# The shared expert's down product moves into the expert loop, and groups of one, two and four experts are spread in the loop

## The reference

```python
h = modulate(rmsnorm(x, norm2_g[l]), sh2, sc2)
idx, wts = route(h, w_router, bias)          # 64 experts, top 8 of each token
routed = sum of silu(h @ w1[e]) * (h @ w3[e]) @ w2[e], weighted, over the chosen e
shared = (silu(h @ s1) * (h @ s3)) @ s2
x = x + g2 * (shared + routed)
```

## Time and profile before

| | us |
|---|---|
| median of 3 runs | 1285.77 (1285.69 to 1286.42) |
| the profiled execution's own time | 1286.71 |
| its span in the trace | 1284.7 |
| PE busy | 1194.7 |
| DVE busy | 363.3 |
| ACT busy | 319.4 |

### The profile page before, as it was taken

The page is one execution under the profiler, slowest core; times in us unless marked ns, Lnnn a source line. Parts: engine busy times, 40 slices in busy tenths (PEclk is TensorE's granted clock), DMA queues, the critical chain, the costliest instruction groups (busy, mean ns, idle before and its releaser), DMA issues.

```text
span 1284.7 us, 16205 instructions
## 1 busy us (share of the span) xinstructions
PE 1194.7 (93%) x6220; PEld 635.2 (49%) x6220; DVE 363.3 (28%) x1140; ACT 319.4 (25%) x570; POOL 10.0 (1%) x44
## 2 busy tenths in 40 slices
PE   5999899999788899999999999999788999999996
PEld 1866447455343444455455747455334444444553
DVE  0495236222112212222124427122112212222124
ACT  1124422222212222222223212222112212222223
POOL 2000000000000000000000000000000000000000
PEclk8899999999888999999999999999889989999998
DMA  9998729899999999999999586699999999999994
GB/s 366 394 416 364 298 80 416 341 391 421 422 421 420 422 420 421 420 421 421 421 422 400 236 331 248 244 392 421 421 422 420 422 420 421 421 420 421 421 421 169
DMA packets 77533, 487.82 MB, mean 380 GB/s; under 512 B 7816, under 2 KB 8968, under 8 KB 23440
## 3 DMA queue, kind: packets, MB, share of 16 engines
q1 hardware_dynamic: 76288, 485.26, 92.1%
q10 hardware_dynamic: 1168, 1.52, 0.3%
HBM read 485.70 MB, written 1.05 MB: 379 GB/s over the span
## 4 chain that ended last, share of the span: by engine, by line
PE 71%; DMA 22%; SPq 3%; DVE 2%; ACT 1%; issue 1%; DVEq 0%; ACTq 0%
PE PS L1347 26%; DMA ring<-in_moe_w 18%; PE PS L1380 10%; PE PS L1296 7%; PE PS L1330 6%; PE PS L1392 5%; PE PS L1317 4%; PE PS L1257 3%; SPq L434 2%; DMA ring<-in_ada_w 2%; PE PS L1475 2%; DMA ring<-in_od_w_in 1%; PE PS L1537 1%; PE PS L1422 1%; PE PS L1405 1%
## 5 line engine op out<-in xcount | busy, mean ns | idle before, releaser
L1347 PE MATMUL PS<-ring,xg 128*32 128x512 f32 (+2 forms) x928 | 206.6, 633 | 26.0 <-DMA ring<-in_moe_w 25.9
L1347 PE MATMUL PS<-ring,xn 128*64 128x512 f32 (+2 forms) x992 | 206.6, 632 | 24.4 <-DMA ring<-in_moe_w 24.4
L1380 PE MATMUL PS<-ring,hidT 128*64 128x512 f32 (+2 forms) x960 | 203.7, 596 | 1.4 <-DVE hidT L1049 1.4
L1347 PEld LDWEIGHTS PS<-ring,xg 128*32 128x32 f32 (+2 forms) x928 | 71.0, 141 | 159.2 <-issue 159.2
L1347 PEld LDWEIGHTS PS<-ring,xn 128*64 128x64 f32 (+2 forms) x992 | 69.2, 137 | 158.8 <-issue 157.3
L1054 DVE SCALAR_TENSOR_TENSOR yl<-PS,wslot,yh 128x1024 fp32r<-128x1024 f32 x58 | 74.4, 1283 | 227.2 <-ACT yh L713 227.2
L1046 DVE TENSOR_TENSOR hid<-PS,hid 128x256 f32<-128x256 f32 x58 | 24.6, 425 | 365.6 <-ACT hid L703 365.6
L1330 PE MATMUL PS<-hot,xh 128*128 128x256 f32 x448 | 126.4, 315 | 1.3 <-ACT xg L689 1.3
L703 ACT ACTIVATE hid<-PS 128x256 f32<-128x256 f32 x58 | 22.3, 385 | 410.3 <-PE PS L1347 399.2
L1380 PEld LDWEIGHTS PS<-ring,hidT 128*64 128x64 f32 (+2 forms) x960 | 64.0, 133 | 99.5 <-issue 92.5
L1330 PE MATMUL PS<-hot,xl 128*128 128x256 f32 x448 | 111.4, 282 | 0.0
(11 more groups left out here) (247 smaller groups left out, 933.5 us busy)
## 6 DMA issues: line engine op xcount, KB each, us to landing
ring<-in_moe_w SPq DMA_DIRECT2D x384, 1024.0 KB, 18.5
ring<-in_ada_w SPq DMA_DIRECT2D x48, 1024.0 KB, 13.0
ring<-in_ev_w_in SPq DMA_DIRECT2D x10, 1024.0 KB, 15.9
ring<-in_sh_w SPq DMA_DIRECT2D x6, 1024.0 KB, 14.4
ring<-in_ev_w_out SPq DMA_DIRECT2D x4, 1024.0 KB, 11.7
ring<-in_od_w_in SPq DMA_DIRECT2D x4, 1024.0 KB, 16.9
ring<-in_od_w_out SPq DMA_DIRECT2D x4, 1024.0 KB, 13.9
x<-in_x SPq DMA_DIRECT2D x1, 1024.0 KB, 5.5
```

Of the source, the lines that this page charges most:

```text
L1347: ins = M(PS[o:o + rows, 6, :], xg[gp][:, k, first_slot + o:first_slot + o + rows], w13[:, :, k, :], start=(k == 0), stop=(k == KD - 1))
L1380: ins = M(PS[o:o + rows, 4 + h, :], hidT[:, m, o:o + rows], slot_view(slots[2][0], 2)[:, m, h * 512:(h + 1) * 512], start=(m == 0), stop=( ...
```

## The change

- The order of the groups becomes P P and then `QWQPPPPWPPPWQWQWWQPWPPQPPW`.
- The shared down product leaves the place before the loop and is done in one piece of 8 matmuls on PE (`shared_down`), before the `up` of group 20 (the 21st). Its tile s2 is no longer loaded before the loop. It takes a place of its own in the list of experts, with kind 2 alone, and is loaded with group 20. So a layer now has 61 places, and `RUN_CELL` becomes cells 1 to 4. The first `scatter` now starts banks 0 to 3.
- The first gather's four parts move up among the routing steps, into banks 7 and 6 in turn. One half of the split of x (`xh` for the second 128 tokens) moves from DVE to ACT. The normalisation of the weights (`weigh`) and the sort come after the first one-hot tables on DVE.
- The block counting on PE (`cumulate`, `make_list`) moves into group 0, `block_list` on DVE behind group 0, and the wait for `ctl_ready` into group 1.
- The loads of groups 2 and 3 are issued in one list, sorted by the time at which their places come free.

```diff
-    for n in range(NARROW // 4):
-        order += [[wide.pop(0)], narrow[4 * n:4 * n + 4]]
-    order += [[wide.pop(0)]]
-    order += [middle[2 * n:2 * n + 2] for n in range(len(middle) // 2)]
-    return order + [[wide.pop(0)]]
+    for kind in "QWQPPPPWPPPWQWQWWQPWPPQPPW":
+        cols, n = {"W": (wide, 1), "P": (middle, 2), "Q": (narrow, 4)}[kind]
+        order.append([cols.pop(0) for _ in range(n)])
+    return order
+SHARED_AT = 20
...
-        EXPERTS = [(g, j) for g in range(NG) for j in range(len(COLUMNS[g]))]
+        EXPERTS = [(g, j) for g in range(NG) for j in range(-(g == SHARED_AT), len(COLUMNS[g]))]
+        SHARED_N = EXPERTS.index((SHARED_AT, -1))
...
-                     + [(("shared", 1, i), NSLOT + i) for i in range(3)])
+                     + [(("shared", 1, i), NSLOT + i) for i in range(2)])
...
+            def load_groups(l, gs, prev):
+
+                who, tiles = {}, []
+                for g in gs:
+                    if g == SHARED_AT:
+                        tiles.append((SHARED_N, 2))
+                    for j, c in enumerate(COLUMNS[g]):
...
+                        tiles += [(n, kind) for kind in range(3)]
+                tiles.sort(key=lambda t: (place_free(*t) if len(gs) > 1 else 0, t[1] == 2))
+                for n, kind in tiles:
+                    s = 3 * (n % CELLS) + kind
+                    if n < CELLS:
+                        wait_occupant(prev[s])
+                    else:
+                        sp.wait_ge(*given_back(l, former(n, kind), kind))
...
-                for g in range(FIXED // 2, NG):
-                    load_group(l, g, prev)
+                load_groups(l, [2, 3], prev)
+                for g in range(4, NG):
+                    load_groups(l, [g], prev)
... ACT, in moe(l)
+                src = x[:, TC - 1, :].rearrange("p (q k) -> p k q", k=KD)
+                nc.scalar.activation(xh[:, TC - 1, :, :], src, ACT.Copy, scale=stat[:, TC - 1:TC]).then_inc(high_ready, 1)
+                load_table(ACT.Silu)
+                act.wait_ge(shared_used, 2 * l + 1)
+                nc.scalar.activation(shs, PS[:, 5, :], ACT.Silu).then_inc(shared_silu, 1)
+                f = main[l]
+                for part in range(2):
+                    gather_out(f, part + 1, 0, part, 7 - part)
                 act.wait_ge(turned_filled, l + 1)
... DVE, in moe(l)
-                sort_experts(l)
+                dve.wait_ge(where_ready, l + 1)
                 for g in range(2):
                     one_hot(g, unsorted).then_inc(f.hot_ready, 1)
-                split_x(l, range(1, TC))
+                weigh(l)
+                sort_experts(l)
                 write_order(l)
+                count_blocks(l)
                 dve.wait_ge(shared_silu, l + 1)
+                dve.wait_ge(shared_filled, l + 1)
... PE, in moe(l)
                 shared_up(1, 0)
+                f = main[l]
+                pe.wait_ge(f.hot_ready, 2)
+                pe.wait_ge(split_ready, TC * (l + 1))
+                gather(f, 0, 0)
                 pe.wait_ge(where_ready, l + 1)
+                gather(f, 0, 1, 6)
...
                 M(PS[0:1, 1, 0:E], number[0:E, :], sort[0:E, :], start=True, stop=True).then_inc(order_filled, 1)
+                for part in range(2, 4):
+                    pe.wait_ge(f.gather_taken, part - 1)
+                    gather(f, 0, part, 9 - part)
                 shared_up(1, 1).then_inc(shared_filled, 1)
...
+                def shared_down():
+
+                    s = 3 * (SHARED_N % CELLS) + 2
+                    pe.wait_ge(landed[s], 16 * (expert_uses[l][s] + turns(SHARED_N, 2)))
+                    wv = slot_view(s, 2)
+                    for b in range(4):
+                        c, h = b // 2, b % 2
+                        for j in range(2):
+                            ins = M(PS[:, b, :], shid[:, j, c * P:(c + 1) * P],
+                                    wv[:, j, h * 512:(h + 1) * 512], start=False, stop=False, skip_group_check=True)
+                    ins.then_inc(shared_used, 1)
... PE, in group(g)
+                    if g == SHARED_AT:
+                        shared_down()
...
+                    if g == 0:
+                        cumulate()
...
+                    if g == 0:
+                        make_list()
+                        pe.wait_ge(shared_hidden, l + 1)
+                    if g == 1:
+                        pe.wait_ge(ctl_ready, l + 1)
```

More of the change, by code:

```diff
@@ L335, in trunk @@
                       + list(zip(ada(1, 1), (4, 5, 14, 10, 11, 0, 1, 2)))
-                      + [(("shared", 0, i), NSLOT + i) for i in range(3)])
+                      + [(("shared", 0, i), NSLOT + i) for i in range(2)])
         odd_units = (list(zip(ada(1, 2, range(4)), (12, 13, 14, 0)))
@@ L368, in placed, with holds, turns, former @@
             return rows
+        def holds(n, kind):
+            return n != SHARED_N or kind == 2
+        def turns(n, kind):
+            return sum(holds(m, kind) for m in range(n % CELLS, n + 1, CELLS))
+        def former(n, kind):
+            return max((m for m in range(n % CELLS, n, CELLS) if holds(m, kind)), default=None)
+        def given_back(l, n, kind):
+            if n == SHARED_N:
+                return shared_used, 2 * l + 2
+            return (main[l].up_filled if kind < 2 else main[l].down_filled), EXPERTS[n][0] + 1
         expert_uses = []
@@ L727, in moe @@
                 nc.scalar.copy(wtsT[0:E, :], PS[0:E, 0, T:2 * T]).then_inc(turned_taken, 1)
[L728 to L732, removed]
+                for part in range(2, 4):
+                    gather_out(f, part + 1, 0, part, 9 - part)
                 def group(g):
@@ L921, in route, with weigh @@
                     take_row(1, 1)
+                split_x(l, range(1, TC))
+            def weigh(l):
                 dve.wait_ge(sel_ready, l + 1)
@@ L1383, in down, with scatter @@
                 ins.then_inc(f.down_filled, 1)
-            def scatter(f, split_at, freed=()):
+            def scatter(f, split_at, freed=(), first=False):
                 freed = list(freed)
@@ L1392, in scatter @@
                             ins = M(PS[:, 2 * c + h, :], hotT[:, c, 0:P], part[:, h * 512:(h + 1) * 512],
-                                    start=False, stop=False, skip_group_check=True)
+                                    start=first and part is yh, stop=False, skip_group_check=True)
                             if freed:
@@ L1513, in moe @@
                 ins.then_inc(sorted_filled, 1)
[L1514 to L1543, removed]
@@ new lines, in cumulate, with make_list @@
+                def cumulate():
+                    pe.wait_ge(count_ready, l + 1)
+                    M(PS[0:E, 2, HB:HB + 1], before[0:E, 0:E], blocks, start=True, stop=False)
+                    M(PS[0:E, 2, HB:HB + 1], ident[0:E, 0:E], blocks, start=False, stop=True).then_inc(cum_filled, 1)
+                def make_list():
+                    pe.wait_ge(over_ready, l + 1)
+                    for t, col in enumerate((ones[0:E, 0:1], ahead)):
+                        ins = M(PS[0:1, 3, 8 + t * LIST:8 + (t + 1) * LIST], col, over[0:E, :], start=True, stop=True)
+                    ins.then_inc(list_filled, 1)
@@ L1550, in group @@
                         slots = [3 * (n % CELLS) + i for i in range(3)]
-                        experts.append([(s, landed[s], 16 * (expert_uses[l][s] + n // CELLS + 1)) for s in slots])
+                        experts.append([(s, landed[s], 16 * (expert_uses[l][s] + turns(n, i))) for i, s in enumerate(slots)])
+                    if g == SHARED_AT:
+                        shared_down()
                     if par == 0:
@@ L1565, in group @@
                     if g:
-                        scatter(f, g, [run_up_free[l][j] for j in range(RUN) if EXPERTS[OWNER[j]][0] == g])
+                        scatter(f, g, [run_up_free[l][j] for j in range(RUN) if EXPERTS[OWNER[j]][0] == g], first=(g == 1))
                     turn_hidden(f, g + 1)
```

60 lines of the change are left out of this document (29 added, 31 removed).

## The result

| | us, median (lowest to highest) | against before |
|---|---|---|
| before | 1285.77 (1285.03 to 1286.62, 9 runs) | 1 |
| after | 1291.89 (1287.96 to 1295.19, 9 runs) | 1.0047, interval 1.0038 to 1.0056 |
| forecast | 1284.2 (1276.5 to 1289.0) | 0.999 |

The kernel is 6 us slower, where I forecast 1.6 us faster. The profiled execution of after took 1289.0 with a span of 1286.9, so it is one of the faster ones of its kernel.

The account below looks back on a forecast made before the run. The DMA stream was taken to bound the loop, with PE some 30 us slack. Layer 1's start +4.6, its loop -5.1 and its run -1.1 sum to -1.6 us, so 1284.2 us from 1285.8; range 1276.5 to 1289.0.

Parts of the forecast that it names:

- the 7.1 of each layer: Late s2 at group 20 delays PE, so the queue later runs empty: 6.1 us, 7.1 with the restart, per layer.
- Before the loop: Stretch up to the first `up`: moved work makes it 8.0 us earlier (bounds 4 to 9.5), worth nothing by itself in layer 0.
- Rival 3: Moved gathers before the loop each wait for ACT or DVE: slower, 1290.2 us with 2 us each; chance 0.1.
- Layer 0: Layer 0's stream: +2.5 + 3.0 + 7.1 - 8.4 = +4.2 us, ending at 687.2 instead of 683.0.
- First spell: Layer 0, after PE's 6.9 us wait at group 2: queue empty 2.0 us, 3.0 with the restart.
- T: The landing time of s2 at group 20, about 7.3 us after PE is ready.
- layer 1's loop: Layer 1's loop from its own start: -8.0, +2.5, +1.0, +7.1 and -7.7, together -5.1 us.
- +1.0: Layer 1's loop: extra time for the queue's restart, 1.0 us.
- -7.7: Layer 1's loop: the 7.7 us of empty queue early in the loop of the kernel before are gained.
- Rivals 1 and 2: No clock loss at groups 2 and 20: 1277.0, chance 0.15; PE never behind at group 20: 1270, 0.08 (half: 1277, 0.12).
- Rival 4: Clock stays low longer, 3.0 us for 2.1 at each wait: slower, 1288 to 1289 us; chance 0.1.
- The rule on a transfer's fixed cost: About 2.0 us fixed per transfer, against the row's 2.4: each empty spell 0.4 shorter, giving an estimated 1282.9 us.

Follow-up runs that it names:

- e1: The changed kernel with tile s2 issued ahead of the four `up` tiles of its group instead of behind them: 1275.08 us, ratio 0.9917.
- e5: The changed kernel with eight useless matmuls on PE ahead of its wait for s2 at group 20: 1286.97 us, ratio 1.0004.
- e0: The changed kernel run again unchanged, for a second profile: 1290.93 us, ratio 1.0031.
- e9: The changed kernel with only one of the eight shared down matmuls left, the wait for s2 kept: 1279.36 us, ratio 0.9943.
- e3: The changed kernel with the group order of the kernel before, shared down product still ahead of group 20: 1286.64 us, ratio 1.0003.
- e6: e1 plus five useless matmuls on PE ahead of layer 0's first `up`: 1273.05 us, ratio 0.989.
- e8: e3 with the shared down product ahead of group 7 and s2 issued ahead of that group's other tiles: 1279.75 us, ratio 0.9949.
- e4: e1 with other slots for layer 1's first ada and projection tiles, so no ada tile waits for the run's down products: 1272.57 us, ratio 0.9892.
- e2: The changed kernel with the shared down product ahead of group 18 instead of group 20: 1276.48 us, ratio 0.9915.

## Why the prediction was wrong

The forecast, cut at the points that both kernels have, against the two profiles of after and e1. For e1 the forecast is the same sum with the 7.1 of each layer taken out. us against before:

| stretch | forecast | after, two profiles | forecast for e1 | e1 |
|---|---|---|---|---|
| start of layer 1's projections | +4.6 | +5.4, +5.9 | -2.5 | -2.1 |
| from there to the first `up` | -8.0 | -8.1, -8.1 | -8.0 | -6.5 |
| from there to the run | +1.8 | +4.9, +7.8 | -5.3 | -3.0 |
| start of layer 1's run | -1.6 | +2.3, +5.6 | -15.8 | -11.6 |

- **Before the loop: right.** -8.0 forecast, -8.05 measured in layer 1; in layer 0 the first `up` began at 215.70 for 224.24. (The terms listed for the stretch add up to 13.4 us and not to 13.2, which makes 7.7; the sum used 8.0.) Rival 3 (stalled gathers) did not happen.
- **Layer 0: right in every piece, a little small.** First spell 3.0 and 3.0; PE's wait at group 2 6.9 and 7.23; at group 20 7.3 and 8.21, then 9.2 and 9.71 of product; dip 7.1 and 7.6, about 60 us behind T. Another 1.1 us were empty ahead of T, which the forecast had at nothing. The stream ended 5.6 later for 4.2, and layer 1 began 5.4 to 5.9 later for 4.6.
- **The step that failed is layer 1's loop**, in the prediction's words "-8.0 for the earlier first `up`, +2.5, +1.0 for the restart, +7.1, -7.7: -5.1", with "The rest is full to the end of the run". The mechanism was right and two terms of the sum were too small. The +1.0 is the restart behind the first `up`, and everything else ahead of group 20 was put at nothing. In e1, which has no dip, the windows give 1.4 us at 805, which is that restart, and 1.1 at 830 and 0.8 at 1000, so 3.3 in all: that is the 2.3 by which e1's loop misses its forecast. The +7.1 for group 20 measured 455.4 - 447.5 = 7.9 in one profile and 458.3 - 447.5 = 10.8 in the other; by the windows it is 7.7 in the dip and 1.2 around T in the former, and 8.5 and 2.8 in the latter. I had let the stream be full whenever my count of slots showed no clear stall. The spells that it left out are short ones at the end of a Q's `up`. In e1 they lie from 832 to 842, where the `up` of group 2 ends at 835.43, and from 1020 to 1030, where that of group 14 (1016.29) ends at 1023.36. Ahead of the latter PE had not waited at all. SP's queue had stood 4.5 us for that `up` to end. So the queue runs empty there because the slots come free late, and not because of a wait of PE just before.
- **The sum closes.** The run of layer 1 begins 3.9 and 7.2 us later than forecast. The forecast for the profiled execution was 1286.7 - 1.6 = 1285.1, which makes 1289.0 and 1292.3; they took 1289.0 and 1292.3.
- **The rivals.** Rivals 1 and 2 did not happen, but e1 is rival 2 made true by one line: 1270 forecast, 1275 measured, and 4.2 of the 5 us between stand in the last two columns (1.5 of them the slow projections after e1's wait of 1.82 us). Rival 4 (the clock low for longer) names the right side and too small a loss: 2.6 and 3.1 us at s2, but the clock also fell at waits of 2.5 us, which I had not counted. e5 puts the clock's whole part at group 20 at 4 us of 15.9.
- **The rule on a transfer's fixed cost.** The ada tile from a nearly empty queue took 4.8 us to land, 2.3 beside its own 2.5, which is close to the row's value (2.4). The Trainium skill, page "DMA: Bandwidth & Descriptors", section "Anatomy of one DMA", has about 2.0 for it, measured on GpSimd's path. The estimate of 1282.9 that goes by it lay farther off than mine.
- **The range** ended at 1289.0. It took its upper end from rivals 3 and 4, one at a time, and no rival moved the sizes of all the empty spells together.

What stays open: why executions of one kernel differ in this. The rows under e0 show where the second profile lost its 3 us, from a wait of 2.55 us on that brought the half clock, but not why that wait was longer than the 1.50 of the first. The spread goes with the late s2 as far as the runs tell: it is 7.2, 4.3, 6.5 and 4.3 us for after, e0, e5 and e9, and 1.6 to 3.7 for before and all the others (4 to 18 runs each). It fits that a lost us of PE goes straight into an empty spell there, while elsewhere a wait absorbs it, but no run shows that by itself.

## What to carry to other kernels

In a loop with an in-order load queue and a ring of slots, a tile that PE needs first must be queued first: here four tiles too late (10 us of stream) gave PE a wait of 8 us, and the queue ran empty some 60 us later, when the ring had come round, far from its cause. Work moved into such a loop belongs where PE waits for the stream by itself (the groups with many tiles), not where the two are level; slack summed over a loop says nothing on a stretch of it (e3). When the count of slots shows PE and the stream within a few us of each other, give each such place (here the end of the `up` of a group with many tiles) an empty spell of about 1 us, and put the range on their sum.

## What the runs showed of the hardware

- The clock can fall after shorter waits than the earlier trace rows let me expect, but not after all of them. After waits of 2.49 and 2.55 us (e0), 2.64 (e6) and 4.26 (e8) the next `up` took 8.77. After 2.37 and 2.58 us (e1), 2.76 (e4), and 3.17 and 3.22 (e2) it took 7.07. So the length of the wait alone does not tell it.
- PEclk is 0.86 over the 35 us around the wait of 8.60 us in e0, and 1.00 in the same stretch of e1. One wait that brought the half clock cost 1.3 to 3.1 us (8.40 for 7.09 at 305.79 in e1, 10.20 for 7.13 in e0).
- The drop follows the wait and hits whatever PE does next: the product (9.71 and 10.20 for 7.13), or, where that is nearly left out, the next `up` (8.59 for 7.09). With useless matmuls in the wait (e5) the product took 7.13, at a gain of 4.0 us.
